# RWKV stage of a two-layer decoder trunk: chunk matrices as 64x64 blocks on quarters of the TensorE array

## The reference, cut to what matters

```python
s_kk = einsum('bhvk,bhk->bhv', state, kk_t)
state = state * w_t - s_kk[..., None] * kka_t + v_t[..., None] * k_t
out   = einsum('bhvk,bhk->bhv', state, r_t)
```

## Time and profile before

| | us |
|---|---|
| median of 3 runs | 3800.9 |
| lowest, highest | 3793.82, 3802.43 |
| profiled execution, its own time | 3806.41 |
| its span | 3804.6 |
| mean granted TensorE clock | 0.959 |

### The profile page before, as it was taken

How to read it: one execution, slowest core, us unless ns; L and a number is a source line. 1 busy time by engine, 2 the same in 40 slices (tenths; PEclk the granted TensorE clock), 3 DMA queues, 4 the chain that set the end, 5 groups by cost and what they waited for, 6 DMA issues and landing times. The chain is left out here.

```text
span 3804.6 us, 63271 instructions
## 1 busy us (share of the span) xinstructions
PE 3490.2 (92%) x20524; PEld 3056.8 (80%) x20524; DVE 2038.7 (54%) x4363; ACT 1478.6 (39%) x3161; POOL 203.8 (5%) x137
## 2 busy tenths in 40 slices
PE   7999978997989999999889999789889899999997
PEld 6787867886879789999777777678778787999996
DVE  3545436553397655555434444265624976555554
ACT  2323224230139555555432322243301485555554
POOL 1101000000000000000011010000100000000000
PEclk9999989998999999999999999799989999999998
DMA  3212122221421555555322212122214215555553
GB/s 111 91 45 91 51 68 78 72 99 40 165 77 68 166 187 187 187 187 187 136 92 73 84 52 84 35 83 72 105 45 149 84 66 184 185 187 186 185 186 120
DMA packets 121925, 432.99 MB, mean 114 GB/s; under 512 B 15712, under 2 KB 18016, under 8 KB 120928
## 3 DMA queue, kind: packets, MB, share of 16 engines
q1 hardware_dynamic: 121824, 431.74, 32.1%
HBM read 430.64 MB, written 1.05 MB: 113 GB/s over the span
## 5 line engine op out<-in xcount | busy, mean ns | idle before, releaser
L236 PE MATMUL bank<-arena,ring 128*128 128x256 f32 x4160 | 999.3, 387 | 44.5 <-PEq L188 13.2
L236 PEld LDWEIGHTS bank<-arena,ring 128*128 128x128 f32 x4160 | 773.4, 194 | 144.6 <-issue 45.4
L1950 DVE TENSOR_TENSOR u_parts<-u_raw,u_parts 128x512 fp32r<-128x512 f32 x384 | 265.8, 693 | 448.7 <-ACT u_parts L1895 448.7
L1895 ACT ACTIVATE u_parts<-u_raw 128x512 fp32r<-128x512 f32 x384 | 242.3, 631 | 519.9 <-PE bank L1834 519.8
L1832 PE MATMUL bank<-xhigh,u_parts 128*128 128x256 f32 x1536 | 433.9, 282 | 1.6 <-DVE u_parts L1950 1.6
L1834 PE MATMUL bank<-xhigh,u_parts 128*128 128x256 f32 x1536 | 434.7, 283 | 0.0
L1833 PE MATMUL bank<-xlow,u_parts 128*128 128x256 f32 x1536 | 434.6, 283 | 0.0
L1832 PE MATMUL bank<-v_parts,act_high 128*128 128x512 f32 x1024 | 407.5, 398 | 13.5 <-DVE v_parts L1955 13.5
L1833 PE MATMUL bank<-v_parts,act_high 128*128 128x512 f32 x1024 | 404.3, 395 | 0.0
L1834 PE MATMUL bank<-v_parts,act_low 128*128 128x512 f32 x1024 | 401.6, 392 | 0.0
L1955 DVE TENSOR_TENSOR v_parts<-v_raw,v_parts 128x512 fp32r<-128x512 f32 x512 | 329.6, 685 | 27.1 <-ACT v_parts L1902 25.2
(11 more groups left out here) (330 smaller groups left out, 5087.2 us busy)
## 6 DMA issues: line engine op xcount, KB each, us to landing
v_raw<-in_v SPq DMA_DIRECT2D x256, 512.0 KB, 3.5
u_raw<-in_u SPq DMA_DIRECT2D x192, 512.0 KB, 4.2
ring<-in_w_side SPq DMA_DIRECT2D x80, 512.0 KB, 3.5
ring<-in_w_gdn SPq DMA_DIRECT2D x64, 512.0 KB, 3.5
ring<-in_w_rwkv SPq DMA_DIRECT2D x48, 512.0 KB, 6.1
ring<-in_w_gdn_side SPq DMA_DIRECT2D x32, 512.0 KB, 3.5
ring<-in_u SPq DMA_DIRECT2D x32, 512.0 KB, 3.6
u_ring<-in_u SPq DMA_DIRECT2D x32, 512.0 KB, 3.5
```

The source lines that it names most:

```text
L236: mm = te.matmul(ps, ring[:, slot, k * P:(k + 1) * P], x[:, k, :], start=(k == 0), stop=(k == KT - 1))
L1895: a_.activation(f32r(u_hi[:, half(n)]), u_raw[:, r % 2, half(n)], ACT.Copy).then_inc(u_high, 1)
L1950: v.tensor_tensor(f32r(u_lo[:, half(n)]), u_raw[:, r % 2, half(n)], u_hi[:, half(n)], ALU.subtract).then_inc(u_low, 1)
```

## The change

All chunk matrices of the RWKV stage (G1, G2, NLM, T_, TT, X) are held as 64x64 blocks: two blocks of a token block lie on partitions 0 to 63 and 64 to 127, four m side by side, 256 columns instead of 512. Each product of 128x128 becomes two products on 64 partitions that write 64 partitions, with 64 columns of weights; the products of the scan use one half of the partitions (the chunk's own). The transposes of TT become products with a 64x64 identity. Masks come from a new constant of 9x64 columns (`consts64`), loaded at the start of each layer's RWKV stage, and `rmask` and `half` are no longer needed. Vh goes, Vt is used by halves. PE increments a semaphore `passed`, which nobody waits for, after its waits, 21 times an iteration. The semaphores of the key products are signalled once for a pair of banks instead of once for a bank.

```diff
+    halves = (slice(0, CH), slice(CH, P))
+    passed = lsem("rwB_passed")
+    def invert64_pe(te, E, S, V, G, i, NLM, T_, TT, X, bX, bY, bYT, levels, fill):
+        view = lambda b: b[:, 0:4 * CH].rearrange("p (m c) -> p m c", m=4)
+        def blocks(out, left, right):
+            for m in range(4):
+                for rows in halves:
+                    mm = te.matmul(view(out)[rows, m], left[rows, m], right[rows, m], start=True, stop=True)
+            return mm
+        for lev in range(1, levels):
...
+            te.wait_ge(*((S.sem, S.at("invT", i)) if lev == 1 else (V.sem, V.at(f"inv{lev - 1}T", i))))
+            te.sem_inc(passed, 1)
+            blocks(bX, NLM[:, lev - 1], T_).then_inc(E.sem, E.one(f"{t}X"))
+            fill(lev, 0)
+            te.wait_ge(S.sem, S.at(f"{t}X", i))
...
+            te.sem_inc(passed, 1)
+            if not last:
+                blocks(bY, TT, X).then_inc(E.sem, E.one(f"{t}Y"))
+            blocks(bYT, X, TT).then_inc(E.sem, E.one(f"{t}YT"))
+            fill(lev, 1)
...
-        Vt, Vh = r_(NB, P), r_(2, NB, P)
-        G1, G2 = r_(4, 2, P), r_(4, 2, P)
-        NLM = r_(5, 4, P)
-        T_, TT, X = r_(4, P), r_(4, P), r_(4, P)
+        Vt = r_(NB, P)
+        G1, G2 = r_(4, 2, CH), r_(4, 2, CH)
+        NLM = r_(5, 4, CH)
+        T_, TT, X = r_(4, CH), r_(4, CH), r_(4, CH)
...
+                sp.dma_start(consts64[:, :], A["consts64"]).then_inc(pload, 16)
                 sp.dma_start(par, A["rwkv_par"][l]).then_inc(pload, 16)
...
+                te.sem_inc(passed, 1)
                 for x, (src, bk) in enumerate(((NBt, (b2, b4)), (KH, (b3, b7)))):
-                    for hh in range(2):
-                        for b in range(NB):
-                            mm = te.matmul(bk[hh][:, b * T:(b + 1) * T], src[rows(hh), b * P:(b + 1) * P],
-                                           KR[rows(hh), b], start=True, stop=True)
-                        mm.then_inc(E.sem, E.one(f"g{x}{hh}"))
+                    for b in range(NB):
+                        for hh, hf in ((0, 0), (1, 1), (0, 1), (1, 0)):
+                            tok = slice(b * P + hf * CH, b * P + (hf + 1) * CH)
+                            mm = te.matmul(bk[hh][rows(hf), b * P:(b + 1) * P].rearrange("p (x c) -> p x c", x=2),
+                                           src[rows(hh), tok], KR[rows(hh), b, :, rows(hf)], start=True, stop=True)
+                    mm.then_inc(E.sem, E.one(f"g{x}"))
...
                 for m in range(4):
-                    mm = te.transpose(b5[:, m * P:(m + 1) * P], TT[:, m], ident)
+                    for hf in range(2):
+                        mm = te.matmul(b5[rows(hf), m * CH:(m + 1) * CH], TT[rows(hf), m], ident64[rows(hf)], start=True, stop=True)
...
-                            mm = te.matmul(b6[:, x * T + b * P + hh * HD:x * T + b * P + hh * HD + HD], G2[:, 2 * hh + b, x],
-                                           Vt[:, b, hh * HD:(hh + 1) * HD], start=True, stop=True)
+                            for hf in range(2):
+                                mm = te.matmul(b6[rows(hf), x * T + b * P + hh * HD:x * T + b * P + hh * HD + HD],
+                                               G2[rows(hf), 2 * hh + b, x], Vt[rows(hf), b, hh * HD:(hh + 1) * HD], start=True, stop=True)
...
-                        te.matmul(b5[:, 0:P], KR[:, b, 0], St, start=True, stop=True).then_inc(E.sem, E.one(f"R{q}"))
+                        te.matmul(b5[rows(hf), 0:P], KR[:, b, 0, rows(hf)], St, start=True, stop=True).then_inc(E.sem, E.one(f"R{q}"))
...
-                        mm = te.matmul(b7[:, hh * HD:(hh + 1) * HD], TT[:, 2 * hh + b], rhs[:, hh * HD:(hh + 1) * HD],
+                        mm = te.matmul(b7[rows(hf), hh * HD:(hh + 1) * HD], TT[rows(hf), 2 * hh + b], rhs[rows(hf), hh * HD:(hh + 1) * HD],
...
-                        te.matmul(b2[:, 0:P], BK[:, 2 + b], Vh[:, hf, b], start=True, stop=False)
-                        te.matmul(b2[:, 0:P], BK[:, b], Um, start=False, stop=True).then_inc(E.sem, E.one(f"S{q}"))
+                        te.matmul(b2[:, 0:P], BK[rows(hf), 2 + b], Vt[rows(hf), b], start=True, stop=False)
+                        te.matmul(b2[:, 0:P], BK[rows(hf), b], Um[rows(hf)], start=False, stop=True).then_inc(E.sem, E.one(f"S{q}"))
...
-                a.activation(T_, b5[:, :].rearrange("p (m c) -> p m c", m=4), ACT.Copy).then_inc(S.sem, S.one("invT"))
+                a.activation(T_, b5[:, 0:4 * CH].rearrange("p (m c) -> p m c", m=4), ACT.Copy).then_inc(S.sem, S.one("invT"))
...
-                    a.activation(Um, b7[:, 0:P], ACT.Copy, scale=half[:, q % 2:q % 2 + 1]).then_inc(S.sem, S.one(f"U{q}"))
+                    a.activation(Um[rows], b7[rows, 0:P], ACT.Copy).then_inc(S.sem, S.one(f"U{q}"))
...
-                        v.tensor_tensor(TT, TT, ident.unsqueeze(1).to_broadcast([P, 4, P]), ALU.add)\
+                        v.tensor_tensor(TT, TT, ident64.unsqueeze(1).to_broadcast([P, 4, CH]), ALU.add)\
...
-                    v.scalar_tensor_tensor(O[:, b], b3[:, 0:P], half[:, hf:hf + 1], O[:, b], ALU.mult, ALU.add)\
-                        .then_inc(V.sem, V.one(f"o{q}"))
+                    v.tensor_tensor(O[rows, b], O[rows, b], b3[rows, 0:P], ALU.add).then_inc(V.sem, V.one(f"o{q}"))
```

More of the change, by code:

```diff
@@ L44 @@
 N_LEVELS = 7
-CONST_COLS = [("ident", P), ("ones", P), ("blk64", P), ("upto", P), ("after", P), ("gmask", 2 * P), ("rmask", 2 * P),
-              ("lmask", N_LEVELS * P), ("restart", T), ("half", 2), ("iota", P)]
+CONST_COLS = [("ident", P), ("ones", P), ("blk64", P), ("upto", P), ("after", P), ("gmask", 2 * P),
+              ("lmask", N_LEVELS * P), ("restart", T), ("iota", P)]
 class Steps:
@@ L133, in _program @@
     gmask = const("gmask", rows=True)
-    rmask = const("rmask", rows=True)
     lmask = const("lmask", rows=True)
     restart = const("restart")
-    half = const("half")
     iota = const("iota")
@@ L411, in invert_levels, with invert64_act, invert64_vec @@
                     fill(lev)
+    halves = (slice(0, CH), slice(CH, P))
[8 more added lines that the diff above has]
+        for lev in range(1, levels):
+            last = lev == levels - 1
+            t = f"inv{lev}"
+            te.wait_ge(G.sem, G.at(f"{t}mask", i))
+            te.wait_ge(*((S.sem, S.at("invT", i)) if lev == 1 else (V.sem, V.at(f"inv{lev - 1}T", i))))
[3 more added lines that the diff above has]
+            te.wait_ge(S.sem, S.at(f"{t}X", i))
+            if lev > 1:
+                te.wait_ge(V.sem, V.at(f"inv{lev - 1}TT", i))
+            te.sem_inc(passed, 1)
[3 more added lines that the diff above has]
+            fill(lev, 1)
+    def invert64_act(a, E, S, i, X, bX, levels, fill):
+        for lev in range(1, levels):
+            a.wait_ge(E.sem, E.at(f"inv{lev}X", i))
+            a.activation(X, bX[:, 0:4 * CH].rearrange("p (m c) -> p m c", m=4), ACT.Copy).then_inc(S.sem, S.one(f"inv{lev}X"))
+            fill(lev)
+    def invert64_vec(v, E, V, i, T_, TT, bY, bYT, levels, fill):
+        view = lambda b: b[:, 0:4 * CH].rearrange("p (m c) -> p m c", m=4)
+        for lev in range(1, levels):
+            if lev < levels - 1:
+                v.wait_ge(E.sem, E.at(f"inv{lev}Y", i))
+                v.tensor_tensor(T_, T_, view(bY), ALU.add).then_inc(V.sem, V.one(f"inv{lev}T"))
+            v.wait_ge(E.sem, E.at(f"inv{lev}YT", i))
+            v.tensor_tensor(TT, TT, view(bYT), ALU.add).then_inc(V.sem, V.one(f"inv{lev}TT"))
+            fill(lev)
     gdn_loaded = [lsem(f"gd_tile{s}") for s in range(4)]
@@ L738, in act_body @@
                 vps = b6[:, 0:2 * P].rearrange("p (b c) -> p b c", b=NB)
-                a.activation(Vt, vps, ACT.Copy).then_inc(S.sem, S.one())
-                for q in range(2):
-                    a.activation(Vh[:, q], vps, ACT.Copy, scale=half[:, q:q + 1]).then_inc(S.sem, S.one("Vt"))
+                a.activation(Vt, vps, ACT.Copy).then_inc(S.sem, S.one("Vt"))
                 act_side(a, i, 0)
@@ L754, in act_body @@
                         a.wait_ge(E.sem, E.at(f"O{q - 1}", i))
-                    a.activation(Um, b7[:, 0:P], ACT.Copy, scale=half[:, q % 2:q % 2 + 1]).then_inc(S.sem, S.one(f"U{q}"))
+                    rows = halves[q % 2]
+                    a.activation(Um[rows], b7[rows, 0:P], ACT.Copy).then_inc(S.sem, S.one(f"U{q}"))
                     if q == 0 and more:
@@ L848, in vec_body @@
                 v.wait_ge(S.sem, S.at("invT", i))
-                invert_levels(None, None, v, None, "inv", E, S, V, G, i, NLM, T_, TT, X, b2, b3, b4, 6, fill)
+                invert64_vec(v, E, V, i, T_, TT, b3, b4, 6, fill)
                 for q in range(T // CH):
                     b, hf = divmod(q, 2)
+                    rows = halves[hf]
                     end = Pp[:, q * CH + CH - 1:q * CH + CH]
@@ L854, in vec_body @@
                         v.wait_ge(E.sem, E.at(f"R{q}", i))
-                        v.tensor_tensor(Rs, b5[:, 0:P], AVO[:, b], ALU.add).then_inc(V.sem, V.one(f"R{q}"))
```

(11 more changed lines are left out.)

32 lines of the change are left out of this document (20 added, 12 removed).

## The result

The changed kernel takes 3665.1 us (median of 4 runs, 3661.8 to 3669.6) against 3798.3 us of the kernel before: ratio 0.965, 95% interval 0.9633 to 0.9667. That is 133 us less, where 80 were forecast and 3680 was the lower end of the range. The two profiled executions lie 144.6 us apart (3806.4 and 3661.8), 11 us more than the medians.

A forecast was written before the change was run, and what follows sets the result against it. PE's stream of work was taken as the bound, busy 92% of the span. -4.4 us per iteration over 14 iterations (-62) and -18 for iteration 7 gave -80, from 3800.9 to 3721 us; range 3680 to 3800.

The forecast's parts named there:

- Levels 1 to 4: Inversion levels in iterations 0 to 6: each takes 3.86 us against 4.68, -3.3 us per iteration.
- Level 5: Last inversion level in iterations 0 to 6, one block less: 3.38 us against 3.8, -0.4 us per iteration.
- L641's block: Start of the front: 32 records in two streams of 16 take 1.96 us against 2.03, -0.1 per iteration.
- rival D: Four quarters run at once in L641's successor (16 us), low-clock stretches vanish (-17): 3688 us; chance 0.13.
- The rest of the front: From L641's block to the first level: both holes close and L657's successor gets shorter, -2.5 us per iteration.
- The scan: Scan steps in iterations 0 to 6: added changes of array form outweigh savings, +1.9 us per iteration.
- The semaphores at 0: 21 separate increments per iteration on PE's queue cost 0 us; highest 0.1 each, 2 us per iteration.
- The price of a record of 128 columns: PE records loading 128 columns of weights cost some 0.11 us whether 128 or 64 columns stream.
- Iteration 7: Last head-loop iteration, without filling: a level takes 3.03 us for 4.74; about -9 us each, -18 in all.
- Rival B: Inversion block halves writing the same PSUM bank take turns, so the kernel gets slower: 3847 us; chance 0.12.
- C: Rival: small records on PE cost 0.085 us instead of 0.060, giving 3783 us; chance 0.15.
- E: Rival: thinner work on the array makes the granted clock fall in every iteration, +34, 3755 us; chance 0.05.

The follow-up runs named there:

- e7: Changed kernel with each of the 21 semaphore increments per iteration on PE's queue made twice: ratio 0.9716 to the kernel before.
- e11: Changed kernel with ACT's copy of each first block made twice, first into a scratch tile: ratio 0.9698 to the kernel before.
- e8: Changed kernel with R and state updates on the whole array, DeltaNet levels' first blocks waiting only for the addition to T_: 3632.1 us, ratio 0.9557.
- e1: Changed kernel with each level's first block again waiting for DVE's addition to TT: 3682 us, ratio 0.9696 to the kernel before.
- e2: Changed kernel with the sixteen key products reordered, in each pair of banks the diagonal quarters first: ratio 0.9659 to the kernel before.
- e4: Changed kernel with three additional DVE products ahead of the first level, making TT late: ratio 0.9863 to the kernel before.
- e6: Changed kernel with R and the state updates on the whole array, Vh and half-masked U as before: ratio 0.9609 to the kernel before.
- e3: Changed kernel with an inversion block's loops swapped, four products of the upper partitions before the lower four: 3744 us, ratio 0.9864.

## Why the prediction was wrong in size

Point by point, by its own steps, per iteration 0 to 6:
- Levels 1 to 4, forecast -3.3: 113.51 to 128.74 is 15.23 us for 18.66, -3.4. Right, with the record at 0.06 and both prices of a change of form. Level 5, forecast -0.4: 3.34 us for 3.85, -0.5.
- L641's block, forecast -0.1: 1.04 us for 2.03, **-1.0**. This term failed. I let two quarters run at a time, as the row pair L616, L617 shows it for two halves, and left four at once to rival D, with a chance of 0.13. 16 us in all.
- The rest of the front, forecast -2.5: from the end of that block to the first level 3.54 us for 5.92, -2.4. Both holes closed. Right.
- The scan, forecast +1.9: 19.43 us (132.08 to 151.51) for 17.80, +1.6. The step of 4.70 is exact; the share ahead of the first R (+0.1 for +0.3) and that after the last (+0.3 for +0.4) were smaller.
- The semaphores at 0: 7 ns for each added one by e7, 0.15 us. The copies' width at nothing in these iterations: shown by e11. Of the other terms put at nothing (masks, O addition, load of constants) none has a run of its own, and what the single increments cost in iteration 7 was not measured either.
- The price of a record of 128 columns, 0.11 us: L385's 1.00 us for eight is 0.125 each. It holds a piece of weight load that stands open; where the wait is fulfilled early it is 0.89 (e8, 579.02 to 579.91), so the price was right.

Sum -5.66 for -4.4: 79 us for 62.

**Iteration 7**, forecast -18, measured -37. Three things are missing in it. I read the new wait of the first block in the diff as the old one: 0.46 us at three boundaries of each, 2.8 us by e1. L641's block gives its 1.0 us here too, 2 us of the 16. And I priced the iteration at the high clock on both sides, though the kernel before spends much of it at 1.2 GHz. Its first levels in the first layer:

```profile
502.01 2.02 PE L385 MATMUL bank<-arena 128*128 128x128 f32 x8
...
509.37 2.05 PE L385 MATMUL bank<-arena 128*128 128x128 f32 x8 [0.87 <-DVE arena L409]
```

A level takes 7.36 us there, and 4.74 at 2.4 GHz. L657 and two such levels cost 6.5 us in the first layer, L657 and three levels 9.5 in the second. The changed kernel loses 1.2 us in each: its iterations 7 take 49.7 and 49.6 us, and the first one of e2, with a clock of 1.00 throughout, 48.5. So 13.6 of the 37 us are the clock. That it rose is shown; what exactly keeps it up is not, and e1, e7 and e11 show how near it is to falling.

**The clock in iterations 0 to 6**, forecast 0, with -17 in rival D: measured -18. I had the condition (the holes ahead of the first level) and left it to a rival, though the forecast itself closed those holes. The granted clock was evidence in the rows; a forecast that closes a hole must also take back what the hole cost in clock. e4 shows that a hole at this place brings the clock down, with a longer one.

So of the 53 us that the forecast lacks, some 32 are the clock (18 and 14), 16 the block of L641, 3 the wait, and the rest small parts of the terms above.

Rival B did not come: both halves of a block write one bank and 16 records take 0.47 us. The Trainium skill ("TensorEngine Tiling (Array Packing)", Gotcha 1) says that different row tiles cannot access the same PSUM bank at once. Here the measurement and the page differ, at least for halves on different partitions, and the measurement decides. C did not come: 0.059 us is what a record of 64 columns takes in its quarter (0.47 us for eight). E did not come. With D's two terms (-16, -17) and the wait (-3) in place the forecast would have been 3685; most of the rest is iteration 7's clock.

## What to carry to other kernels

Price a change of array form and count them: here each costs 0.15 to 0.20 us, more than a 64x64 product takes, and making R and the state updates larger but of their neighbour's form (e6) gained 1.0 us an iteration. Where a hole in PE's work ends, look at the granted clock behind it: closing 1.4 us of holes went with 1.3 us of clock per iteration on average, and a stretch without cover, like iteration 7, can jump by 11 to 15 us when its levels grow by 0.3 to 0.5 us (e1, e7, e11). What costs nothing under cover can cost there: an increment on PE's queue was 7 ns in iterations 0 to 6 and 0.16 us at a wait of iteration 7. When a wait is moved to another operand of the same loop, follow which engine it stood for: one such line was worth 22 us in the kernel before.

## What the runs showed of the hardware

- Products on all four 64x64 quarters of the array stream at once: 32 records of 128 columns in 1.04 us, where one after the other at 0.11 us they would take 3.5.
- Two halves that write the same PSUM bank on different partitions overlap, as L616 and L617 do with different banks: 16 records of 64 columns in 0.47 us.
- The order of issue matters for longer runs: with four records per quarter before the other pair of quarters next to nothing is lost (e2, +0.04 us), with eight in a row on one half the other half starts about five records late (e3, 0.28 us a block).
- An added increment on PE's queue costs 7 ns on average in the covered iterations, and 0.16 us where PE stands at a wait (e7).
